# A two-block transformer on one core: memory weights, memory products and the x path reordered in the first phase

## The chip, the cores and the metric

The kernel runs on one core of a Trainium2 chip. The metric is device time in microseconds (us) of one launch, the median of several runs. The core has TensorE (PE in the profile, its weight loads PEld), VectorE (DVE), ScalarE (ACT), GpSimd (POOL) and SyncE (SP), each with a queue of instructions of its own, worked off in order. DMAs are issued from the queues of SP, ACT and POOL.

## What is computed

A transformer layer with two attentions, then two more layers on its output, which also attend to a memory of 256 tokens. All of it in fp32, 512 tokens of 1024 features. What lies in the first phase is only this:

```python
mod = silu(c) @ w_ada + b_ada                     # 6 x 1024 columns
shift_mix, scale_mix, gate_mix, shift_ffn, scale_ffn, gate_ffn = split(mod, 6)
h = rms_norm(x) * (1 + scale_mix) + shift_mix     # 512 x 1024
proj = h @ w_in                                   # 1024 x 3072
...
# for each of two later layers l, from mem (256 x 1024):
kv_l = (rms_norm(mem) * mem_norm_l) @ w_mem_kv_l  # 1024 x 512, keys and values
```

The rest (attentions, output projections, three feed-forward parts with convolutions) is not touched by the change.

## The kernel before, in words

Features lie on the partitions in 8 tiles of 128, tokens on the columns. A matrix product with 32-bit precision is made of three passes: each weight chunk of 128 x 2048 is split into a high part (`w_hi`, by ACT, L1479) and the rest (`w_lo`, by DVE, L1921), the activations likewise into `act_hi` and `act_lo`, and for each tile of inputs PE adds hi*hi, hi*lo and lo*hi (L808 to L810). A chunk is 256 output columns, so 2 output tiles of 8 input tiles, 48 matmuls. The chunks are numbered through the whole kernel; chunk 0 is the first of `w_in`.

The order of the work is written out by hand: each engine has a program, and semaphores say when a step may start. The first phase goes as follows.

- **SP** (L462 to L510) loads `mem`, then half of the small vectors (L439), then `x` in one DMA of 2 MB (L465), then the first 256 columns of the memory weights (`load_mem(0)`, 1 MB, L468). It then waits for the third slab of `w_ada` (`ada_loaded[2]`, L503) and loads chunks 0 and 1 (L457). Chunk 2 goes into a stage that w_ada used, and waits for its first two adds of the second group (`ada_added` of 10, L452).
- **POOL** (L611 to L656) builds the identity, waits until the small vectors are turned and copied (L633), issues four loads of `w_ada` of 1 MB, builds the constants (L638, L647), waits for chunk 0 (L649), issues four more, then parks the scaled memory of both layers in DRAM (2 MB, L655) and loads small things.
- **ACT** squares the two memory tiles (L1683), takes the root, and the silu of `c`. For each of 8 feature tiles of the turned memory it writes two copies out of PSUM, each with the gain of one layer (`mem_scaled`, L1698). The root for x stands between two of them (L1695). Then it copies the 8 turned tiles of x into `x_norm` (L1703), splits chunk 0 (L1479), and makes `act_hi` (L1713).
- **DVE** makes the diagonal matrices of the memory's inverse norms (L2210), waits for `x`, makes its four sums of squares (L2225), the reciprocal (L2270) and four diagonals (L2273). It adds up the first eight parts of `w_ada` (L2238, L2241), sums the turned columns (L2279), adds bias and one (L2282), and from there goes on without a choice: `w_lo` of chunk 0 (L1921), eight `act_lo` (L2289), the memory's keys (L2263), `w_lo` of chunk 1, eight more adds of `w_ada`, a copy of the first output (L2255), `w_lo` of chunk 2, and the shifted activations (L2295). The shift is known only later than the scale: chunks 0 and 1 use the scaled activations, and what the shift adds to them is summed apart (L2371).
- **PE** turns the memory, 8 tiles, by products with the diagonal that also scale it (L1093). Two banks of PSUM are used in turn, so that each tile waits for ACT's copies of the last but one (L1100). It turns x likewise (L1093 again), and waits for the last copy. It does a quarter of the memory's key products (`mem_half`, L1122), turns the columns of `w_ada`'s sums (`ada_sum`, L1073), does the other three quarters, and begins chunk 0 as soon as its weights and the first `act_lo` are there. Inside chunk 1 stands the sum for the shift (L1148), behind it four tiles of the raw x (L1110), behind chunk 2 the vectors of the convolutions (L921).

`mem_half(0, 0)` and `mem_half(0, 1)` are the two tiles of keys for the memory, 16 instructions each.

## Time and profile before

| | us |
|---|---|
| median of 3 runs | 1817.51 (1817.28 to 1817.79) |
| the profiled execution, its own time | 1817.18 |
| its span in the profile | 1815.5 |
| PE busy | 1780.8 (98% of the span) |
| DVE busy | 1096.0 (60%) |
| ACT busy | 733.0 (40%) |
| POOL busy | 40.4 (2%) |

The profile is taken from one execution. The span is from its first to its last instruction; the execution's own time is 1.7 us more. Busy time is what an engine spends in instructions that compute; matmuls overlap, and a matmul's duration is longer than the distance to the next. The first phase, up to the point at which PE has no gap any more, is about 73 us of the 1815.5.

### The profile page before, as it was taken

Reading aid. Unit: us, or ns where it says so; the run is one execution under the profiler, and the core shown is the slowest. Engines: PE = TensorE matmul, PEld = TensorE weight load, DVE = VectorE, ACT = ScalarE, POOL = GpSimd, SP = SyncE. Lnnn points to the kernel's source line nnn. Section 1 sums busy time; section 2 is a strip of 40 time slices with the busy share of each in tenths; the row PEclk is TensorE's granted clock in tenths of the full one; section 3 lists DMA queues with packets and bytes.
Section 4 is the critical chain, followed back from the end, with each engine's and each line's share of the span. In section 5 each row is a group of like instructions: output and inputs, shape, how many; then the busy total and the mean of one; then the engine's idle time right before and its main releaser. Section 6 shows DMA issues by size and latency. Waiting matters only on the chain.

```text
span 1815.5 us, 22458 instructions
## 1 busy us (share of the span) xinstructions
PE 1780.8 (98%) x8312; PEld 1427.9 (79%) x8312; DVE 1096.0 (60%) x1601; ACT 733.0 (40%) x1031; POOL 40.4 (2%) x78
## 2 busy tenths in 40 slices
PE   7999899999999999999999999999999999999998
PEld 6887556788888888878888888889765788888887
DVE  6877675655555335765677674245577567767423
ACT  7313663343344223444334433232365443443322
POOL 4110000000000000000000000000000000000000
PEclk9999999999999999999999999999999999999999
DMA  9793112223322323312322222233401233222231
GB/s 348 268 336 129 47 53 97 77 94 108 99 92 87 106 86 100 109 47 93 114 94 92 92 92 96 95 93 99 163 24 47 70 108 100 92 92 92 93 105 70
DMA packets 149081, 195.29 MB, mean 108 GB/s; under 512 B 3646, under 2 KB 133000, under 8 KB 146332
## 3 DMA queue, kind: packets, MB, share of 16 engines
q1 hardware_dynamic: 141272, 155.28, 26.0%
q0 software_dynamic: 7600, 39.13, 5.8%
q8 instruction: 41, 0.67, 0.2%
q14 instruction: 20, 0.16, 0.0%
q10 hardware_dynamic: 148, 0.05, 0.0%
HBM read 189.15 MB, written 5.29 MB: 107 GB/s over the span
## 4 chain that ended last, share of the span: by engine, by line
PE 91%; DVE 5%; ACT 2%; issue 1%; DMA 1%; ACTq 0%; DVEq 0%
PE bank L808 20%; PE bank L810 20%; PE bank L809 20%; PE bank L871 3%; PE bank L873 2%; PE bank L872 2%; PE bank L1452 2%; PE bank L1453 2%; PE bank L1451 2%; PE bank L995 1%; PE bank L947 1%; PE bank L964 1%; PE bank L851 1%; PE bank L852 1%; PE bank L853 1%
## 5 line engine op out<-in xcount | busy, mean ns | idle before, releaser
L1921 DVE TENSOR_TENSOR w_lo<-w_stage,w_hi 128x2048 fp32r<-128x2048 f32 (+3 forms) x135 | 296.6, 2197 | 439.1 <-ACT w_hi L1479 438.8
L808 PE MATMUL bank<-act_hi,w_hi 128*128 128x512 f32 x1232 | 482.6, 392 | 2.2 <-DVE act_lo L1971 0.7
L810 PE MATMUL bank<-act_hi,w_lo 128*128 128x512 f32 x1232 | 480.0, 390 | 0.0
L809 PE MATMUL bank<-act_lo,w_hi 128*128 128x512 f32 x1232 | 479.9, 390 | 0.0
L1479 ACT ACTIVATE w_hi<-w_stage 128x2048 fp32r<-128x2048 f32 (+3 forms) x137 | 251.7, 1837 | 459.6 <-PE bank L810 334.7
L808 PEld LDWEIGHTS bank<-act_hi,w_hi 128*128 128x128 f32 x1232 | 231.4, 188 | 53.4 <-DVE act_lo L1971 2.3
L810 PEld LDWEIGHTS bank<-act_hi,w_lo 128*128 128x128 f32 x1232 | 231.4, 188 | 48.2
L809 PEld LDWEIGHTS bank<-act_lo,w_hi 128*128 128x128 f32 x1232 | 231.5, 188 | 47.8 <-issue 0.5
L809 PE MATMUL bank<-mid_lo,w_hi 128*128 128x512 f32 x352 | 137.1, 389 | 0.0
L810 PE MATMUL bank<-mid_hi,w_lo 128*128 128x512 f32 x352 | 137.1, 389 | 0.0
L808 PE MATMUL bank<-mid_hi,w_hi 128*128 128x512 f32 x352 | 137.1, 389 | 0.0
L1624 ACT ACTIVATE mid_hi<-tmp 128x512 f32 x66 | 40.7, 633 | 98.4 <-DVE tmp L2131 98.4
L809 PEld LDWEIGHTS bank<-mid_lo,w_hi 128*128 128x128 f32 x352 | 66.1, 188 | 13.8
L808 PEld LDWEIGHTS bank<-mid_hi,w_hi 128*128 128x128 f32 x352 | 66.1, 188 | 13.6
L810 PEld LDWEIGHTS bank<-mid_hi,w_lo 128*128 128x128 f32 x352 | 66.1, 188 | 13.6
L1451 PE MATMUL bank<-w_hi,mid_hi 128*128 128x512 f32 x176 | 68.9, 392 | 0.0
L1453 PE MATMUL bank<-w_lo,mid_hi 128*128 128x512 f32 x176 | 68.6, 390 | 0.0
L1452 PE MATMUL bank<-w_hi,mid_lo 128*128 128x512 f32 x176 | 68.6, 390 | 0.0
L1616 ACT ACTIVATE tmp<-tmp,vec 128x512 f32<-128x512 f32 x44 | 33.5, 809 | 70.0 <-DVE tmp L1943 70.0
L1616 ACT ACTIVATE mid_val<-tmp,vec 128x512 f32 x44 | 33.5, 808 | 69.7 <-DVE tmp L1943 69.7
L1943 DVE SCALAR_TENSOR_TENSOR tmp<-bank,rms 128x512 f32<-128x512 f32 x88 | 56.3, 681 | 0.0
L2135 DVE TENSOR_TENSOR mid_lo<-tmp,mid_hi 128x512 f32 x66 | 42.7, 689 | 9.3 <-ACT mid_hi L1624 9.3
(412 smaller groups left out, 2608.6 us busy)
## 6 DMA issues: line engine op xcount, KB each, us to landing
ada_stage<-in_w_ada POOLq DMA_DIRECT2D x24, 1024.0 KB, 7.6
w_stage<-in_w_up SPq DMA_DIRECT2D x22, 1024.0 KB, 5.0
w_stage<-in_a_ffn_in SPq DMA_DIRECT2D x22, 1024.0 KB, 5.0
w_stage<-in_b_ffn_in SPq DMA_DIRECT2D x22, 1024.0 KB, 5.0
w_stage<-in_w_in SPq DMA_DIRECT2D x10, 1024.0 KB, 7.7
w_stage<-in_b_ffn_out SPq DMA_DIRECT2D x10, 1024.0 KB, 5.1
w_stage<-in_w_down SPq DMA_DIRECT2D x8, 1024.0 KB, 5.1
w_stage<-in_a_ffn_out SPq DMA_DIRECT2D x8, 1024.0 KB, 5.0
```

Of the source, the lines that this page charges most:

```text
L808: pe.matmul(dst, wh, mh, start=start and k == 0, stop=False)
L809: pe.matmul(dst, wh, ml, start=False, stop=False)
L810: last = pe.matmul(dst, wl, mh, start=False, stop=stop and k == nk - 1)
L871: pe.matmul(dst, wh, mh, start=start and k == ks[0], stop=False)
L1451: pe.matmul(dst, mh, hi[:, k, :], start=j == 0 and k == 0, stop=False)
L1452: pe.matmul(dst, ml, hi[:, k, :], start=False, stop=False)
L1453: last = pe.matmul(dst, mh, lo[:, k, :], start=False, stop=j == 5 and k == nk - 1)
L1479: act.activation(w_hi[slot][:, 0:n], raw[:, 0:n], ACT.Copy).then_inc(w_hi_done, 1)
L1616: act.activation(conv_tile(f, i, s, m), conv_src(f, s, m)[:, :], ACT.Identity, scale=w2, bias=b).then_inc(tap_started, 1)
L1921: dve.tensor_tensor(w_lo[slot][:, 0:n], raw[:, 0:n], w_hi[slot][:, 0:n].bitcast(FP32), ALU.subtract).then_inc(w_ready, 1)
L1943: return dve.scalar_tensor_tensor(out=dst, in0=src[:, :], scalar=scale, in1=norm[:, :], op0=ALU.mult, op1=ALU.mult)
L2135: dve.tensor_tensor(mid_lo[:, bass.ds(2 * i + m, 1), :], tmp[:, m, :], mid_hi[:, bass.ds(2 * i + m, 1), :].bitcast(FP32), ALU.subtract).th ...
```

## The change

- **SP**: the first memory weights are loaded ahead of `x`, and `x` comes in two DMAs of 1 MB (tokens 0 to 255, then 256 to 511), each with a semaphore of its own.
- **POOL**: the first four loads of `w_ada` wait for the first half of `x` too.
- **PE**: the memory is turned into banks 0 to 3, two tiles in each, with no wait between them. All memory products (`mem_half`) stand right behind, as soon as layer a's copies are kept. Then x is turned (banks 0 to 3), then the sums of the modulation.
- **ACT and DVE**: DVE keeps the turned memory for layer a (8 multiplies), ACT for layer b (8 activations, tiles 4 to 7 first, then 0 to 3). Each waits for pairs of tiles, and for the other engine where both would read one bank. Of the four sums of squares of x ACT makes two (token tiles 0 and 2), behind its keeping, and DVE two (1 and 3), behind its own. The four diagonals go from DVE to ACT.
- **The first split** (chunk 0) is made in two halves of 1024 columns, which are input tiles 0 to 3 and 4 to 7. PE starts with the first (`w_half`), and waits for the second before the fifth input tile. DVE makes the second half of `w_lo` behind the third `act_lo`.
- The semaphores `x_turned`, `xn_turned` and the memory's part of `tr_ready` become one, `turned`. The scratch for the squares of x moves from `x` to the space of `act_hi`.

```diff
@@ -82,7 +82,7 @@
 CONVS = [("conv_w", "conv_b"), ("a_ffn_conv_2", "a_ffn_conv_b_2"), ("b_ffn_conv_2", "b_ffn_conv_b_2")]
 
 
-BATCHES = [("vec", 1), ("mem", 8), ("conv", 2), ("ws", 1),
+BATCHES = [("vec", 1), ("conv", 2), ("ws", 1),
            ("out", 8)]
 TR0 = {name: sum(n for _, n in BATCHES[:i]) for i, (name, _) in enumerate(BATCHES)}
 
...
@@ -239,7 +239,7 @@
         q_bias = stats[:, 24:28]
         bias_acc = tmp[:, 1, :]
         col_1, col_2, col_12 = stats[:, 36:40], stats[:, 40:44], stats[:, 56:60]
-        x_junk = x[:, 6:8, :].rearrange("p a b -> p (a b)")
+        x_junk = at("x_junk", [P, NT, D], o_act)
         sq = tmp[:, 2:4, :]
 
 
...
@@ -251,6 +251,9 @@
 
         def mem_bank(c, m):
             return (4 + m, 6 + m, 6 + m, 4 + m)[c]
+
+        def xn_bank(k):
+            return bank[k % 4]
 
         def norm_bank(name):
             return bank[6] if name == "oa" else bank[5]
...
@@ -365,12 +367,14 @@
         c_act = sem("c_act")
         mod_summed, mod_added, mod_ready = sem("mod_summed"), sem("mod_added"), sem("mod_ready")
         ada_turned, ada_reduced, kb_saved = sem("ada_turned"), sem("ada_reduced"), sem("kb_saved")
+        mem_kept = [sem(f"mem_kept{l}") for l in range(2)]
+        w_half = sem("w_half")
         mem_ss, mem_root, mem_rms = sem("mem_ss"), sem("mem_root"), sem("mem_rms")
         mem_diag, mem_tile, mem_done, mem_saved = (
             sem("mem_diag"), sem("mem_tile"), sem("mem_done"), sem("mem_saved"))
         w_mem_loaded = [sem(f"w_mem_loaded{c}") for c in range(4)]
         x_squared, x_root, x_inv, x_diag = sem("x_squared"), sem("x_root"), sem("x_inv"), sem("x_diag")
-        xn_turned, xn_saved = sem("xn_turned"), sem("xn_saved")
+        xn_saved = sem("xn_saved")
         v_tile, v_saved = sem("v_tile"), sem("v_saved")
         mem_stored, mem_back = sem("mem_stored"), sem("mem_back")
         mem_parked, mem_unparked = sem("mem_parked"), [sem(f"mem_unparked{l}") for l in range(2)]
...
@@ -462,13 +466,16 @@
             sp.dma_start(mem_tok[:, :, :], a["mem_2"][0].rearrange("(t p) d -> p t d", p=P))\
                 .then_inc(mem_loaded, 16)
             load_vectors(sp, VECTORS[0::2])
-            sp.dma_start(x_tok[:, :, :], a["x"][0].rearrange("(t p) d -> p t d", p=P))\
-                .then_inc(x_loaded, 16)
+
             def load_mem(c):
                 sp.dma_start(w_mem[c][:, :, :], cols(rows("a_w_mem_kv_2"), 0, KT, CHUNK_COLS * c))\
                     .then_inc(w_mem_loaded[c], 16)
 
             load_mem(0)
+            for h in range(2):
+                sp.dma_start(x_tok[:, 2 * h:2 * h + 2, :],
+                             a["x"][0, 2 * P * h:2 * P * (h + 1), :].rearrange("(t p) d -> p t d", p=P))\
+                    .then_inc(x_loaded[h], 16)
 
             def stream(ph, w, pairs):
 
...
@@ -631,6 +638,7 @@
             pool.memset(eps, EPS).then_inc(consts_set, 1)
             pool.memset(one_col, 1.0).then_inc(consts_set, 1)
             pool.wait_ge(tr_saved, TR0["vec"] + 1)
+            pool.wait_ge(x_loaded[0], 16)
             for n in range(4):
                 ada(n, first[n])
             ones = [(neg_upper, -1.0), (tri, 1.0), (strict_neg, 0.0), (causal_neg, 0.0), (ident_b, 0.0)]
...
@@ -786,9 +795,12 @@
         @block.tensor
         def _(pe):
             def chunk(c, slot, nk, ncol, moving, g=None, gslot=0, start=True, stop=True, n=SEQ,
-                      k0=0, tile_wait=None, chunk_wait=None, between=None, inside=None):
-
-                pe.wait_ge(w_ready, c + 1)
+                      k0=0, tile_wait=None, chunk_wait=None, between=None, inside=None, halves=False):
+
+                if halves:
+                    pe.wait_ge(w_half, 2)
+                else:
+                    pe.wait_ge(w_ready, c + 1)
                 if start and (not isinstance(g, int) or g >= 2):
                     pe.wait_ge(group_free, g - 1)
                 if chunk_wait:
...
@@ -1095,12 +1109,10 @@
 
             pe.wait_ge(mem_diag, 2)
             for k in range(KT):
-                n = TR0["mem"] + k
-                if n >= 2:
-                    pe.wait_ge(tr_saved, n - 1)
                 for t in range(2):
-                    last = scaled_turn(bank[6 + n % 2], mem_tok[:, t, P * k:P * (k + 1)], NT + t)
-                last.then_inc(tr_ready, 1)
+                    last = scaled_turn(bank[k // 2][:, NMEM * (k % 2):NMEM * (k % 2) + NMEM],
+                                       mem_tok[:, t, P * k:P * (k + 1)], NT + t)
+                last.then_inc(turned, 1)
 
             def turn_x(tiles):
                 for k in tiles:
...
@@ -1109,7 +1121,7 @@
                     for t in range(NT):
                         last = pe.transpose(bank[4 + k % 4][:, P * t:P * (t + 1)],
                                             x_tok[:, t, P * k:P * (k + 1)], ident[:, :])
-                    last.then_inc(x_turned, 1)
+                    last.then_inc(turned, 1)
 
             def mem_half(c, m, ks=range(KT)):
                 l = c // 2
...
@@ -1125,23 +1137,22 @@
                     last.then_inc(mem_done if m else mem_tile, 1)
 
 
+            pe.wait_ge(mem_kept[0], KT)
+            pe.wait_ge(w_mem_loaded[0], 16)
+            mem_half(0, 0)
+            mem_half(0, 1)
             pe.wait_ge(x_diag, NT)
+            pe.wait_ge(mem_kept[1], KT)
             for k in range(KT):
-                if k == 2:
-                    pe.wait_ge(tr_saved, TR0["mem"] + KT)
                 if k >= 4:
                     pe.wait_ge(xn_saved, k - 3)
                 for t in range(NT):
-                    last = scaled_turn(bank[4 + k % 4], x_tok[:, t, P * k:P * (k + 1)], t)
-                last.then_inc(xn_turned, 1)
+                    last = scaled_turn(xn_bank(k), x_tok[:, t, P * k:P * (k + 1)], t)
+                last.then_inc(turned, 1)
             pe.wait_ge(xn_saved, KT)
-            pe.wait_ge(w_mem_loaded[0], 16)
-            mem_half(0, 0, range(4))
             pe.wait_ge(consts_set, 14)
             pe.wait_ge(ada_added, 8)
             ada_sum(range(8, 16), 2)
-            mem_half(0, 0, range(4, KT))
-            mem_half(0, 1)
             def shift_sum():
                 pe.wait_ge(ada_added, 16)
                 pe.wait_ge(group_free, G0["qk_a"] + 1)
...
@@ -1151,7 +1162,7 @@
                 chunk(C0["qk_a"] + j, j % 2, KT, CHUNK_COLS, act, g=G0["qk_a"] + j, gslot=j % 2,
                       tile_wait=normed(("w_in_scaled", "", "w_in", "")[j]) if j % 2 == 0 else None,
                       chunk_wait=(scaled, SPLIT0["w_in_scaled"] + 8) if j == 1 else None,
-                      inside=shift_sum if j == 1 else None)
+                      inside=shift_sum if j == 1 else None, halves=j == 0)
                 if j == 1:
                     pe.wait_ge(mem_saved, 1)
                     turn_x(range(4))
...
@@ -1689,25 +1700,42 @@
             act.wait_ge(tr_saved, TR0["vec"] + 1)
             act.activation(sig_c, vec[:, VEC0["c"]:VEC0["c"] + 8], ACT.Silu).then_inc(c_act, 1)
             act.preload_act_table(ACT.Sqrt)
+            def keep_mem_b(k):
+                act.wait_ge(turned, 2 * (k // 2) + 2)
+                if k < 4:
+                    act.wait_ge(mem_kept[0], 2 * (k // 2) + 2)
+                act.activation(mem_scaled[:, 1, k, :], bank[k // 2][:, NMEM * (k % 2):NMEM * (k % 2) + NMEM],
+                               ACT.Copy, scale=gain("b_mem_norm_2", k)).then_inc(mem_kept[1], 1)
+
             for k in range(KT):
-                if k == 6:
-                    act.wait_ge(x_squared, NT)
-                    act.activation(x_rms, x_ss, ACT.Sqrt, scale=1.0 / D, bias=eps).then_inc(x_root, 1)
-                act.wait_ge(tr_ready, TR0["mem"] + k + 1)
-                for l, name in enumerate(("a_mem_norm_2", "b_mem_norm_2")):
-                    last = act.activation(mem_scaled[:, l, k, :], bank[6 + (TR0["mem"] + k) % 2][:, 0:NMEM],
-                                          ACT.Copy, scale=gain(name, k))
-                last.then_inc(tr_saved, 1)
+                keep_mem_b((k + 4) % KT)
+            for t in (0, 2):
+                act.wait_ge(x_loaded[t // 2], 16)
+                act.activation(x_junk[:, t, :], x_tok[:, t, :], ACT.Square, accum_out=x_ss[:, t:t + 1])\
+                    .then_inc(x_squared, 1)
+            act.wait_ge(x_squared, NT)
+            act.activation(x_rms, x_ss, ACT.Sqrt, scale=1.0 / D, bias=eps).then_inc(x_root, 1)
+            act.wait_ge(x_inv, 1)
+            for t in range(NT):
+                act.activation(diag[:, t, :], ident[:, :], ACT.Copy, scale=x_rms[:, t:t + 1]).then_inc(x_diag, 1)
+
+            def save_xn(k):
+                act.wait_ge(turned, KT + k + 1)
+                act.activation(x_norm[:, k, :], xn_bank(k)[:, :], ACT.Copy).then_inc(xn_saved, 1)
+
             for k in range(KT):
-                act.wait_ge(xn_turned, k + 1)
-                act.activation(x_norm[:, k, :], bank[4 + k % 4][:, :], ACT.Copy).then_inc(xn_saved, 1)
+                save_xn(k)
+            act.wait_ge(xn_saved, KT)
 
             def save_x(tiles):
                 for k in tiles:
-                    act.wait_ge(x_turned, k + 1)
+                    act.wait_ge(turned, 2 * KT + k + 1)
                     act.activation(x[:, k, :], bank[4 + k % 4][:, :], ACT.Copy).then_inc(x_saved, 1)
 
-            split_at(0)
+            act.wait_ge(w_loaded[0], 16)
+            for half, done in ((0, w_half), (1, w_hi_done)):
+                act.activation(w_hi[0][:, 1024 * half:1024 * half + 1024],
+                               w_stage[0][:, 1024 * half:1024 * half + 1024], ACT.Copy).then_inc(done, 1)
             act.wait_ge(scaled, SPLIT0["w_in_scaled"] + 8)
             for t in range(KT):
                 act.activation(act_hi[:, t, :], x_norm[:, t, :], ACT.Copy, scale=modv(SCALE_MIX, t))\
...
@@ -2216,13 +2244,16 @@
             last.then_inc(tr_saved, 1)
             dve.wait_ge(tr_saved, TR0["vec"] + 1)
             dve.tensor_tensor(gain_a1, vec[:, VEC0["final_g"]:VEC0["final_g"] + 8],
-                              vec[:, VEC0["a_norm1_2"]:VEC0["a_norm1_2"] + 8], ALU.mult)\
-                .then_inc(gain_a1_set, 1)
-            dve.wait_ge(x_loaded, 16)
-            for t in range(NT):
-                if t:
-                    dve.wait_ge(x_squared, t)
-                dve.tensor_tensor_reduce(out=x_junk, in0=x_tok[:, t, :], in1=x_tok[:, t, :], scale=1.0,
+                              vec[:, VEC0["a_norm1_2"]:VEC0["a_norm1_2"] + 8], ALU.mult)
+            for k in range(KT):
+                dve.wait_ge(turned, 2 * (k // 2) + 2)
+                if k >= 4:
+                    dve.wait_ge(mem_kept[1], 2 * (k // 2) - 2)
+                dve.tensor_scalar(mem_scaled[:, 0, k, :], bank[k // 2][:, NMEM * (k % 2):NMEM * (k % 2) + NMEM],
+                                  gain("a_mem_norm_2", k), None, ALU.mult).then_inc(mem_kept[0], 1)
+            for t in (1, 3):
+                dve.wait_ge(x_loaded[t // 2], 16)
+                dve.tensor_tensor_reduce(out=x_junk[:, t, :], in0=x_tok[:, t, :], in1=x_tok[:, t, :], scale=1.0,
                                          scalar=0.0, op0=ALU.mult, op1=ALU.add,
                                          accum_out=x_ss[:, t:t + 1]).then_inc(x_squared, 1)
 
...
@@ -2268,10 +2299,6 @@
 
             dve.wait_ge(x_root, 1)
             dve.reciprocal(x_rms, x_rms).then_inc(x_inv, 1)
-            dve.wait_ge(x_inv, 1)
-            for t in range(NT):
-                dve.tensor_scalar(diag[:, t, :], ident[:, :], x_rms[:, t:t + 1], None, ALU.mult)\
-                    .then_inc(x_diag, 1)
             dve.wait_ge(c_act, 1)
             for n in range(4):
                 ada_first(n)
...
@@ -2281,7 +2308,13 @@
             dve.wait_ge(mod_added, 1)
             dve.scalar_tensor_tensor(out=mod[:, 8:16], in0=mod[:, 8:16], scalar=1.0, in1=vec[:, P + 8:P + 16],
                                      op0=ALU.add, op1=ALU.add).then_inc(scaled, 8)
-            split_w(0, 0)
+            def split_first(half):
+                dve.wait_ge(w_hi_done if half else w_half, 1)
+                part = slice(1024 * half, 1024 * half + 1024)
+                dve.tensor_tensor(w_lo[0][:, part], w_stage[0][:, part], w_hi[0][:, part].bitcast(FP32),
+                                  ALU.subtract).then_inc(w_ready if half else w_half, 1)
+
+            split_first(0)
             dve.wait_ge(scaled, SPLIT0["w_in_scaled"] + 8)
 
             def low_scaled(t):
...
@@ -2306,6 +2339,8 @@
 
             for t in range(KT):
                 low_scaled(t)
+                if t == 2:
+                    split_first(1)
             mem_group(0)
             split_w(1, 1)
             for n in range(4, 8):
```

## Rows read from the trace of the kernel before

**Rows 1.** Windows: us, length, busy (x instructions) of PE, PEld, DVE, ACT, POOL, clock, DMA.
```profile
30.00:40.00 10.00, 10.00 (x48) 8.57 (x47) 9.54 (x14) 9.79 (x13) 9.96 (x18) 1.00 0.92 344
...
100.00:130.00 30.00, 30.00 (x134) 24.87 (x133) 21.55 (x13) 4.79 (x3) 3.17 (x6) 1.00 1.00 363
```

**Rows 2.** Chain that ended last, 0 to 130 us: start, us, what.
```profile
44.23 8.99 DMA ada_stage<-in_w_in
```

**Rows 3.** Timeline of PE, 8 to 73 us: start, us, what.
```profile
9.50 2.07 PE L1093 MATMUL bank<-diag,mem_tok 128*128 128x128 f32 x8 [0.62 <-DVE diag L2210]
12.45 6.07 PE L1093 MATMUL bank<-diag,mem_tok 128*128 128x128 f32 x24 [0.88 <-ACT mem_scaled L1698]
19.05 7.41 PE L1093 MATMUL bank<-diag,x_tok 128*128 128x128 f32 x64 [0.53 <-DVE diag L2273]
27.15 2.00 PE L1122 MATMUL bank<-mem_scaled,w_mem 128*128 128x256 f32 x8 [0.69 <-ACT x_norm L1703]
29.25 1.07 PE L1073 MATMUL bank<-ident,ada_acc 128*128 128x128 f32 x8
30.15 5.35 PE L1122 MATMUL bank<-mem_scaled,w_mem 128*128 128x256 f32 x24
35.14 0.58 PE L808 MATMUL bank<-act_hi,w_hi 128*128 128x512 f32 x1
...
37.41 0.39 PE L808 MATMUL bank<-act_hi,w_hi 128*128 128x512 f32 x1
...
60.51 0.47 PE L808 MATMUL bank<-act_hi,w_hi 128*128 128x512 f32 x1 [0.57 <-DVE act_lo L2295]
...
71.51 0.62 PE L921 MATMUL bank<-ident,vec_rows 88*128 88x88 f32 x6
72.46 0.47 PE L808 MATMUL bank<-act_hi,w_hi 128*128 128x512 f32 x1 [0.33 <-DVE qkv L2255]
```

**Rows 4.** Timeline of DVE, 8 to 56 us.
```profile
12.51 1.22 DVE L2225 CUSTOM_DVE_ANT_0 x_res<-x_tok 128x1024 f32<-128x1024 f32 x1 [2.58 <-DMA x_tok<-in_x]
...
17.90 0.18 DVE L2270 RECIPROCAL stats<-stats 128x4 f32<-128x4 f32 x1 [0.36 <-ACT stats L1695]
...
18.91 0.75 DVE L2238 TENSOR_SCALAR ada_acc<-ada_stage,stats 128x1024 f32<-128x1024 f32 x1
19.69 9.41 DVE L2241 SCALAR_TENSOR_TENSOR ada_acc<-ada_stage,stats,ada_acc 128x1024 f32<-128x1024 f32 x7
...
31.77 2.28 DVE L1921 TENSOR_TENSOR w_lo<-w_stage,w_hi 128x2048 fp32r<-128x2048 f32 x1
33.97 5.38 DVE L2289 SCALAR_TENSOR_TENSOR act_lo<-x_norm,vec,act_hi 128x512 fp32r<-128x512 f32 x8
39.28 0.74 DVE L2263 COPY kmT<-bank 128x256 f32<-128x256 f32 x2
...
55.20 2.29 DVE L1921 TENSOR_TENSOR w_lo<-ada_stage,w_hi 128x2048 fp32r<-128x2048 f32 x1 [1.21 <-ACT w_hi L1479]
```

**Rows 5.** Timeline of ACT, 5 to 45 us.
```profile
7.25 1.06 ACT L1683 ACTIVATE sq_junk<-mem_tok 128x1024 f32<-128x1024 f32 x1
...
13.71 1.69 ACT L1698 ACTIVATE mem_scaled<-bank,vec 128x256 f32<-128x256 f32 x4 [0.58 <-PE bank L1093]
...
17.57 0.30 ACT L1695 ACTIVATE stats<-stats 128x4 f32<-128x4 f32 x1
...
29.77 1.91 ACT L1479 ACTIVATE w_hi<-w_stage 128x2048 fp32r<-128x2048 f32 x1 [2.68 <-DMA w_stage<-in_w_in]
```

**Rows 6.** DMA issues from 3.5 to 5 us: KB each, median us to landing.
```profile
x_tok<-in_x SPq DMA_DIRECT2D x1, 2048.0 KB, 8.7
w_mem<-in_a_w_mem_kv SPq DMA_DIRECT2D x1, 1024.0 KB, 12.9
```

**Rows 7.** PE matmuls of mem_tok: groups by form, 9 to 17.75 us; then by tile.
```profile
L1093 PE MATMUL bank<-diag,mem_tok 128*128 128x128 f32 x28 | 7.5, 444 | 1.7 <-ACT mem_scaled L1698 0.9 <-DVE diag L2210 0.6
...
L1093 PE MATMUL bank<-diag,mem_tok x32: 275/422/583, 9.5 to 18.2; 128*128 128x128 f32 x32
```

10 lines of the change are left out of this document (6 added, 4 removed).

## The prediction

> **What bounds the kernel now.** Read the windows first: from 100 to 130 us TensorE has no gap, from 30 to 40 it is already full [rows 1]. Whatever starts the stream of 512-column products earlier or later therefore moves the end, unless a later wait takes it up. The only such place nearby is in the chain of waits: the load of the third weight chunk, 44.23 to 53.22 us [rows 2].
>
> Then the timeline of TensorE [rows 3]: memory tiles turned from 9.50 to 18.52 with gaps, x turned from 19.05 to 26.46, a quarter of the memory products, the sums of the modulation at 29.25, the other three quarters from 30.15, the first chunk at 35.14. At 60.51 the third chunk starts after 0.57 of waiting for act_lo, and at 72.46 the fourth after 0.33 of waiting for a copy by VectorE.
>
> The timeline of VectorE [rows 4] says what 29.25 waited for: the eight adds of w_ada, which run without a gap from 18.91 to 29.10. Then come reduction, w_lo of the first chunk (31.77), act_lo (33.97) and so on without a pause until 53.99; then 1.21 us of idle before w_lo at 55.20. So two chains, VectorE's and TensorE's, lie within a microsecond of each other. The end moves only by what both are late, less these idle times.
>
> **The change, part by part.** I take four engine queues in their new order.
>
> *Turning the memory.* The same 32 instructions go to four banks, without waiting for ScalarE. Their pace depends on TensorE's clock. 28 of them, begun before 17.75, average 444 ns; the fastest, after it, takes 275 [rows 7]. That is the low level (1.2 GHz) against the high one (2.4). At the low level the pace is (2.07 - 0.58) / 7 = 0.213 us, at the high one 7.41 / 64 = 0.116 [rows 3, 7]. The windows' column calls the granted clock 1.00 in both [rows 1], so durations decide here. In the old order the rise came at 17.8, after a stream with gaps. The new stream has no gap, so 17.8 is the late end; the early end is 9.5, the high level from the first turn on. Neither row is nearer, and I take the middle, 13.65. By then 19 have begun; the other 13 take 1.5. The sixth tile is ready at 14.5, the eighth at 15.4.
>
> *Keeping it.* ScalarE takes all eight tiles for layer b, beginning with the fifth, at 1.69 / 4 = 0.42 each [rows 5]: tiles 5 and 6 until 15.35, 7 and 8 until 16.25, 1 to 4 until 17.95. VectorE takes eight for layer a. A multiply of 128x256 out of PSUM isn't in the trace; the copy of that size is, 0.74 for two [rows 4], and the bound above is ScalarE's 0.42. At 0.37, behind ScalarE's pair in the same bank, the last two end at 17.0. At the upper bound it is 17.1.
>
> *Memory products.* All 32 now come before x is turned. At 5.35 / 24 = 0.223 [rows 3] they take 7.1: 17.05 to 24.15. They fill some idle time, but most of them now stand before a step on the path.
>
> *Squares of x.* These wait behind the keeping. VectorE's two take 2 x 1.26 (four had 12.51 to 17.54 [rows 4]): 17.0 to 19.5. ScalarE's two take 1.18 each (7.25 to 8.40 is one [rows 5]): 17.95 to 20.3. Root and reciprocal add 0.55 (17.57 to 18.1 [rows 4, 5]), so the adds of w_ada begin at 20.9, not 18.91. VectorE saves the four diagonals, 0.8 between 18.08 and 18.91, and that is already in it. The adds take 10.2 and end at 31.1. The four diagonals on ScalarE have no row: between 0.3 (the root, four columns) and 0.42 (256 columns) each [rows 5], done by 22.6, covered by the memory products until 24.15.
>
> *Turning x.* 8.1 from the first turn to TensorE free again (19.05 to 27.15, with ScalarE's last save [rows 3]): 24.15 to 32.25. The sums of the modulation therefore begin at 32.2, not 29.25: **2.95 late**, and TensorE is now what is last (w_ada is ready at 31.1).
>
> *First split in halves.* VectorE's work until the fourth act_lo is the same: w_lo of 2.20 (31.77 to 33.97) and four at 5.38 / 8 = 0.67. In the old order the fourth was there at 36.66 and TensorE asked for it at 37.41 [rows 3, 4], with 0.75 to spare, because the memory products had held the start until 35.14. In the new one it comes at 36.66 + 2.95 = 39.6 and TensorE, which starts at 36.55 (a half of w_lo saved), stands before it at 38.8. So the halving starts the first product 1.1 earlier and gives back 0.8 at the fourth tile. From there TensorE is 2.95 - 0.7 = 2.25 late.
>
> *What takes it up.* VectorE is 2.95 late from act_lo on, and the 1.21 of idle before 55.20 goes: 1.75. TensorE is 2.25 late, and the wait of 0.57 before 60.51 goes: 1.7. Both meet at the third chunk; the fourth is again tied to VectorE's copy [rows 3]. **Sum: +1.75 us.** Nothing later has slack for it: TensorE is full.
>
> *Transfers.* x and the memory weights landed 12.46 and 17.1 us in [rows 6]. In the new order the second megabyte in SyncE's queue is the first half of x. So it lands near 12.5, and the last half by 17.1, before 19.1, where ScalarE wants it. GpSimd's four loads of w_ada wait for the first half, 12.6 instead of 10.03. Behind them on GpSimd's queue stand the constants, wanted only at 32.2. The bounds are no delay (the bus had the same volume) and 2.6 in full. Even then the fourth slab, used in the old order at 26.5, is wanted at 28.6. The first weights, landed before 29.77 [rows 5], come at 32.4 at the latest, and ScalarE is free for them at 32.2. The parking of the memory is needed at 55. Cost 0, up to the third chunk's load, which is a rival below.
>
> **How the numbers follow.** The profiled run has a span of 1815.5, 1.7 around it, 0.3 below the median. 1815.5 + 1.75 = 1817.25, with 1.7 and 0.3 around it 1819.3. A microsecond on the start of the sums is a microsecond on the end, above a delay of 1.2. The rise at 17.8 gives 33.6, so +3.15; at 9.5 it gives 30.3, so 0. Less than 0.2% (3.6 us) counts as no change.
>
> **The rivals.**
> - *A, slower: the clock is still low when the memory products begin.* They then stand at 18.45, after a pause of 1.7 for the keeping, and each costs 0.22 more. With eight of 32 at the low level: 4.35 + 1.8 - 1.2 = +4.95, 1822.5; with all 32, 1827.7. It decides from the third slow product on. For it: 28 turns ran low in the trace [rows 7]. Against: the stream is denser. 0.13.
> - *B: the third weight chunk lands late.* It is asked for 2.95 later, at 47.2, and VectorE can take it from 56.95, so it decides when the load takes over 7.8. The row says 8.99 [rows 2], but beside the parking, which is nearly over by then. Landed at 56.2, VectorE is 2.95 late: +2.95, 1820.5. 0.17.
> - *C: nothing moves.* With the clock high from the start the sums begin 1.05 late and all of it is taken up: 1817.5. 0.12.
> - *D: halves of x land one after another with their full latency.* The Trainium skill (DMA: Bandwidth & Descriptors, Bandwidth) gives 6.15 us for one megabyte alone and asks for at least that size. By an estimate from this page, x would be there at 24.5 and the end come near +6. The trace has three megabytes in 11.1 us behind the first [rows 6], 3.7 each, overlapped, so it speaks against this rule here. From rows, D is a last half that lands after 19.1, at one for one: at 22 the adds begin at 23.7 and end at 33.9, +3.45, 1821.0. 0.04.
> - *E, faster.* The products that held the start at 35.14 are gone, and if the squares were done by 18 the sums could begin where they did; both chains would then gain at most the 0.5 between act_lo at 34.65 and 35.14, and again lose it to the load of rows 2. Over 0.2% I see no mechanism: 0.04, within it part of C.
> The forecast (+0.8 to +3.2) has 0.50. Faster 0.04, same 0.79, slower 0.17 (A, half of the tail of D, part of B). The range reaches from C, 1817.2, to most of A, 1822.4.
>
> **What would show it.** Right: x turned only from about 24 on, the sums of the modulation at 31.5 to 33.6, TensorE last before them; VectorE idle before the reduction; the fourth act_lo waited for in the first chunk; no idle of VectorE before the third w_lo; 72.46 moved by 1.75. Wrong: x turned before 22, or the sums before 30.5.

## The result, and the profile after

| us | before | changed |
|---|---|---|
| median of 21 runs each | 1817.67 | 1821.59 |
| lowest, highest | 1816.83, 1820.39 | 1819.67, 1823.83 |
| ratio, 95% interval | | 1.002 [1.0014, 1.0026] |
| span of the profiled execution | 1815.5 | 1817.8 |

Slower by 3.9 us, just above the 3.6 that was called a change. The profiled span is only 2.3 longer. The 21 times fall into two groups with nothing between: a first of ten from 1819.67 to 1820.35, an upper one of eleven from 1821.59 to 1823.83. The median is the lowest time of the upper group, so one run more in the first group would have put it near 1820.4. The profile is of the first group.

One run of all that follow, in e3_no_pool_wait, took 2684.23 us at a mean granted clock of 0.62; it enters no comparison, and its cause is not known.

TensorE's timeline in it, to be laid beside [rows 3]:

```profile
9.53 5.25 PE L1107 MATMUL bank<-diag,mem_tok 128*128 128x128 f32 x32 [0.33 <-DVE diag L2238]
16.70 7.17 PE L1134 MATMUL bank<-mem_scaled,w_mem 128*128 128x256 f32 x32 [1.91 <-DVE mem_scaled L2252]
23.71 7.31 PE L1107 MATMUL bank<-diag,x_tok 128*128 128x128 f32 x64
31.70 1.10 PE L1087 MATMUL bank<-ident,ada_acc 128*128 128x128 f32 x8 [0.69 <-ACT x_norm L1724]
36.29 0.65 PE L822 MATMUL bank<-act_hi,w_hi 128*128 128x512 f32 x1 [3.49 <-DVE act_lo L2322]
...
40.01 0.39 PE L822 MATMUL bank<-act_hi,w_hi 128*128 128x512 f32 x1
...
60.67 1.91 PE L1122 MATMUL bank<-ident,x_tok 128*128 128x128 f32 x16
62.84 0.47 PE L822 MATMUL bank<-act_hi,w_hi 128*128 128x512 f32 x1 [0.25 <-DVE act_lo L2328]
...
74.79 0.47 PE L822 MATMUL bank<-act_hi,w_hi 128*128 128x512 f32 x1 [0.34 <-DVE qkv L2286]
```

The memory is turned without gaps, the products stand at 16.70, x follows at 23.71 (19.05 before), and the sums of the modulation begin at 31.70, 2.45 late. Then comes what the kernel before does not have: 3.49 us of idle before the first chunk at 36.29. Up to 39.7 the products behind it take 0.63 each, with 0.43 from one to the next; from 40.01 on they take 0.39, 0.23 apart. The fourth tile's product begins at 40.01 against 37.41, and the fourth chunk at 74.79 against 72.46: 2.33 late.

The third chunk, where the kernel before had waited 0.57, still waits 0.25. Ahead of it TensorE turns four tiles of the raw x, from 60.67 on. The same step in the kernel before:

```profile
58.03 1.91 PE L1110 MATMUL bank<-ident,x_tok 128*128 128x128 f32 x16
```

So TensorE ends its second chunk 2.64 late, and the 0.57 of waiting would have left 2.07 of that. VectorE's timeline, beside [rows 4]:

```profile
11.65 0.88 DVE L2252 TENSOR_SCALAR mem_scaled<-bank,vec 128x256 f32<-128x256 f32 x2 [1.69 <-PE bank L1107]
...
19.66 0.75 DVE L2269 TENSOR_SCALAR ada_acc<-ada_stage,stats 128x1024 f32<-128x1024 f32 x1
...
34.26 1.22 DVE L2314 TENSOR_TENSOR w_lo<-w_stage,w_hi 128x1024 fp32r<-128x1024 f32 x1
...
37.39 1.22 DVE L2314 TENSOR_TENSOR w_lo<-w_stage,w_hi 128x1024 fp32r<-128x1024 f32 x1
38.52 3.40 DVE L2322 SCALAR_TENSOR_TENSOR act_lo<-x_norm,vec,act_hi 128x512 fp32r<-128x512 f32 x5
...
57.52 2.29 DVE L1949 TENSOR_TENSOR w_lo<-ada_stage,w_hi 128x2048 fp32r<-128x2048 f32 x1 [0.96 <-ACT w_hi L1490]
```

The adds of w_ada begin at 19.66 (18.91 before) and end at 30.16, so they were not what the sums waited for. The halves of w_lo are there (34.26, 37.39). The fourth act_lo is ready at 39.2, before TensorE wants it. And VectorE still stands idle before the third w_lo, 0.96 at 57.52.

GpSimd's loads of w_ada, and the third weight chunk in the chain of waits, beside [rows 2]:

```profile
13.88 3.00 POOL L618 DMA_DIRECT2D ada_stage<-in_w_ada  x4 [12.26 <-DMA x_tok<-in_x]
...
31.93 2.85 POOL L618 DMA_DIRECT2D ada_stage<-in_w_ada  x4 [11.36 <-DMA w_stage<-in_w_in]
```

```profile
46.80 8.75 DMA ada_stage<-in_w_in
```

The first four are issued at 13.88 instead of 10.03, the next four at 31.93 instead of 30.04. The third weight chunk is asked for at 46.80 instead of 44.23 and lands at 55.55 instead of 53.22.

Two chains meet at the third chunk. One is the transfer: load, w_hi, w_lo, sum of the shift, `act_hi`, `act_lo`. From the landing to TensorE's third chunk it is 7.29 us in both profiles (60.51 less 53.22, 62.84 less 55.55). The other is TensorE itself, whose second chunk must be done before `act_hi` can be written again. ScalarE's `act_hi` shows which came last; here it was the sum (L2338), so the transfer:

```profile
61.18 5.02 ACT L1756 ACTIVATE act_hi<-x_norm,vec 128x512 fp32r<-128x512 f32 x8 [3.69 <-DVE vec L2338]
```

The landing is 2.33 late and so is the fourth chunk; TensorE alone would have made it 2.07.

### The profile page after: what moved, and what is told of

The parts are those of the page before. It is cut to its first block, busy times and chain, and to the rows that moved or that the text cites. A ratio compares the mean times of both kernels' runs of the same rounds, so it can differ in the third digit from the quotient of the medians.

```text
span 1817.8 us, 22473 instructions
## 1 busy us (share of the span) xinstructions
PE 1779.6 (98%) x8312; PEld 1426.0 (78%) x8312; DVE 1096.4 (60%) x1602; ACT 733.2 (40%) x1032; POOL 39.0 (2%) x78
## 4 chain that ended last, share of the span: by engine, by line
PE 91%; DVE 5%; ACT 2%; issue 1%; DMA 1%; ACTq 0%; DVEq 0%
PE bank L822 20%; PE bank L824 20%; PE bank L823 20%; PE bank L885 3%; PE bank L887 2%; PE bank L886 2%; PE bank L1464 2%; PE bank L1463 2%; PE bank L1462 2%; PE bank L1009 1%; PE bank L961 1%; PE bank L978 1%; PE bank L865 1%; PE bank L866 1%; PE bank L867 1%; PE bank L1060 1%
## 5 line engine op out<-in xcount | busy, mean ns | idle before, releaser
L1949 DVE TENSOR_TENSOR w_lo<-w_stage,w_hi 128x2048 fp32r<-128x2048 f32 (+2 forms) x134 | 294.5, 2197 | 439.8 <-ACT w_hi L1490 439.6
```

The costliest lines, as they stand in the source:

```text
L1949: dve.tensor_tensor(w_lo[slot][:, 0:n], raw[:, 0:n], w_hi[slot][:, 0:n].bitcast(FP32), ALU.subtract).then_inc(w_ready, 1)
```

## The experiments

Theories: the **queue** (memory products ahead of the turning of x make the sums late), the **transfers** (everything from w_ada on lands later), the **clock** (new idle stretches of TensorE let its clock fall, in some executions more than in others). "Fourth chunk" is its first product in the profiled execution: 72.46 before, 72.19 in another execution of the kernel before (1816.86). The number behind a label is the median. None of the experiments differs from the kernel before by 2%, and "late" always means against the first profile of the kernel before.

**r0_changed**: the changed kernel once more, no edit.

> The changed kernel again, beside the others on one chip. If the spread of its times (1819.7 to 1823.8 in the first result) belongs to the kernel, it comes back: some runs near 1820, others 2 to 4 us above, median 3 to 4 us over the kernel before. If it belonged to that chip, the median is about 2.3 over (the difference of the two profiled spans) and the runs lie within 1 us.

1822.58, ratio 1.0023 [1.0014, 1.0031]. Four runs from 1819.53 to 1820.29, seven from 1822.51 to 1823.71: the groups belong to the kernel. The profiled one, of the first group, has its fourth chunk at 74.41.

**e1_half_behind**

```diff
             mem_half(0, 0)
-            mem_half(0, 1)
             pe.wait_ge(x_diag, NT)
...
             ada_sum(range(8, 16), 2)
+            mem_half(0, 1)
```

> The changed kernel with the second half of the memory products (16 instructions, 3.6 us) put back behind the sums of the modulation. Queue theory (the products stand before the turning of x and make it late): x is turned from 21.1, when its diagonals are there, not from 23.7; the sums begin at 30.2, when the adds of w_ada end, not at 31.7. Clock theory (TensorE's 3.5 us of idle before the first chunk lets its clock fall, and how much of the next work runs low differs from run to run): the idle is gone, no product of the first chunk takes 0.63, and the runs lie within 1 us of each other near 1820. Transfer theory (the third weight chunk lands at 55.5 because all transfers from w_ada on are 1.7 to 1.9 late): the profiled fourth chunk still starts at 74.4 to 74.8. If the queue alone made the loss, it starts at 73.2 and the median falls to about 1818.5.

1820.36, ratio 1.0014 [1.0006, 1.0023], from 1818.91 to 1822.68: one broad group. TensorE's timeline:

```profile
17.83 5.41 PE L1134 MATMUL bank<-mem_scaled,w_mem 128*128 128x256 f32 x16 [1.91 <-DVE mem_scaled L2252]
...
31.12 1.07 PE L1087 MATMUL bank<-ident,ada_acc 128*128 128x128 f32 x8 [0.73 <-ACT x_norm L1724]
...
73.81 0.47 PE L822 MATMUL bank<-act_hi,w_hi 128*128 128x512 f32 x1 [0.34 <-DVE qkv L2286]
```

Sixteen products took 5.41, not the 3.6 they take later in the same run, so x was turned two microseconds later than expected and the sums began at 31.12, not 30.2. This is the first sight of the low clock in the memory products. The expectation named only the idle before the first chunk; there no product took 0.63, but the spread stayed; the pause of 1.91 ahead of the products was still there. The fourth chunk at 73.81 is below the 74.4 expected by the transfers alone. Its load was asked for at 46.17 and landed at 54.56, a microsecond earlier than in the changed kernel, and the fourth chunk is late by the same 1.35 as the landing.

**e2_keep_busy**

```diff
             ada_sum(range(8, 16), 2)
+            for n in range(14):
+                pe.transpose(bank[6 + n // 7][:, 0:P], ident[:, :], ident[:, :])
```

> The changed kernel with 14 turns of the identity, whose output nobody reads, in TensorE's idle before the first chunk (3.1 us at the high level); all else as it is. Clock theory: the first products take 0.39, not 0.63, all runs lie near 1820 (within 1 us), and the median is 1 to 2 us under the changed kernel's, though work was added. Queue and transfer theory alone: nothing changes in time or in spread, since both chains are later at the third chunk (the profiled fourth chunk at 74.7 as now).

1821.83, ratio 1.0018 [1.0009, 1.0027], 1819.98 to 1822.63. A miss as it was built: the 14 turns took 1.69, not 3.1, and left 1.96 of idle:

```profile
33.03 1.69 PE L1157 MATMUL bank<-ident 128*128 128x128 f32 x14
36.68 0.47 PE L822 MATMUL bank<-act_hi,w_hi 128*128 128x512 f32 x1 [1.96 <-DVE act_lo L2324]
...
37.83 0.63 PE L823 MATMUL bank<-act_lo,w_hi 128*128 128x512 f32 x1
```

The first three products ran high, the next ones low. It neither showed the clock theory nor refuted it: the times are one range up to 1822.63, not two groups, but the median fell by 0.75 only.

**e3_no_pool_wait**

```diff
             pool.wait_ge(tr_saved, TR0["vec"] + 1)
-            pool.wait_ge(x_loaded[0], 16)
```

> The changed kernel without GpSimd's wait for the first half of x ahead of the four loads of w_ada (issued at about 10.0, not 13.9). Transfer theory: the slabs land up to 1.7 us earlier, the first weights before 30, the third weight chunk near 53.8, VectorE has no idle before the third w_lo (0.96 now) and the fourth chunk starts at 73.8: 0.9 us gained. If the transfers cost nothing, as the prediction had it, the fourth chunk stays at 74.7. The other side: x's second half then shares the bus with w_ada and lands after 17, and the squares and with them the adds start up to 1 us later.

1819.97, ratio 1.0014 [1.0006, 1.0023]. That median counts the run of 2684.23; the other eleven have 1819.88, and eight of them lie from 1819.64 to 1820.19. VectorE's third w_lo, and ScalarE's act_hi for the third chunk:

```profile
57.02 2.27 DVE L1948 TENSOR_TENSOR w_lo<-ada_stage,w_hi 128x2048 fp32r<-128x2048 f32 x1
```

```profile
61.45 5.02 ACT L1755 ACTIVATE act_hi<-x_norm,vec 128x512 fp32r<-128x512 f32 x8 [5.83 <-PE bank L823]
```

VectorE has no idle before w_lo any more, as expected: the load landed near 53.7, 0.45 late, though it was asked for at 47.33, 3.1 late. So GpSimd's wait for x is what made the landing late in the changed kernel. But the profiled fourth chunk, at 75.05, did not come forward: act_hi for the third chunk also waits until TensorE has finished the second, and TensorE was 3.2 late there (its clock fell before the first chunk, as in the changed kernel). This tie between the chains was not in the prediction. Whether more runs fell into the first group by this edit or by chance stays open.

**e7_fill_both**

```diff
+            for n in range(8):
+                pe.transpose(bank[7][:, 0:P], ident[:, :], ident[:, :])
             pe.wait_ge(mem_kept[0], KT)
...
             ada_sum(range(8, 16), 2)
+            for n in range(28):
+                pe.transpose(bank[6 + n // 14][:, 0:P], ident[:, :], ident[:, :])
```

> The changed kernel with TensorE kept busy in both of its new idle stretches by turns of the identity whose output nobody reads: 8 between the turning of the memory and the memory products (1.91 us of idle now), 28 between the sums of the modulation and the first chunk (3.49 us; 14 of them took 1.69). Clock theory: no product of the memory and of the first chunk runs at the low level's pace, and the upper group of times (1822.5 to 1823.7, 7 of 11 runs) is gone: all runs between 1819.4 and 1820.6. The profiled fourth chunk stays at 74.4 to 74.8, since VectorE and the third weight load are there as late. If the two groups have another cause, they stay and the median is 1822 or more.

1819.92, ratio 1.0011 [1.0002, 1.002]. All eleven runs from 1819.76 to 1820.33. Adding 36 instructions that compute nothing took 2.7 us off the median and the upper group away.

```profile
17.39 7.17 PE L1134 MATMUL bank<-mem_scaled,w_mem 128*128 128x256 f32 x32 [1.04 <-DVE mem_scaled L2256]
...
36.98 0.47 PE L822 MATMUL bank<-act_hi,w_hi 128*128 128x512 f32 x1 [0.43 <-DVE act_lo L2326]
...
40.01 0.50 PE L822 MATMUL bank<-act_hi,w_hi 128*128 128x512 f32 x1 [0.72 <-DVE act_lo L2326]
...
74.86 0.47 PE L822 MATMUL bank<-act_hi,w_hi 128*128 128x512 f32 x1 [0.33 <-DVE qkv L2290]
```

The products take 7.17, no product of the first chunk takes 0.63, and now the wait for the fourth tile shows (0.72 at 40.01) that the prediction had put there. The fourth chunk, 74.86, is as late as in the changed kernel. The rise of the clock came as late here as in executions of the upper group (the memory was turned in 6.13 us, see below), and still the products ran high. l1_look, of the same series and the same chip, took 1823.59 without the fillers. So the idle ahead of the products lets the clock fall, the clock is the difference between the groups, and queue and transfers are what is left. Which of the two fillers did it was not tried by itself; the next profiles point to the first.

**l1_look, l3_look_changed**: two more executions of the changed kernel.

> One more execution of the changed kernel, to find one of the upper group in a profile. Clock theory: if its time is above 1822, more of its first chunk or of its memory products runs at the low level's pace (0.43 for a 512-column product, not 0.23) than in the two profiles of the lower group (9 of the first 10 products). If its time is near 1820, it looks like these.

> A further execution of the changed kernel. Clock theory: above 1822, the windows show the low level (near 0.5) in the memory products and at the start of the first chunk, as in the slow profile (sums at 34.3); near 1820, the products run high (sums at 31.6 to 31.8) and only the start of the first chunk is low.

1823.59 and 1822.55, both of the upper group. TensorE in the first:

```profile
9.52 6.18 PE L1107 MATMUL bank<-diag,mem_tok 128*128 128x128 f32 x32 [0.34 <-DVE diag L2238]
17.62 8.86 PE L1134 MATMUL bank<-mem_scaled,w_mem 128*128 128x256 f32 x32 [1.92 <-DVE mem_scaled L2252]
...
34.31 1.10 PE L1087 MATMUL bank<-ident,ada_acc 128*128 128x128 f32 x8 [0.69 <-ACT x_norm L1724]
38.89 0.77 PE L822 MATMUL bank<-act_hi,w_hi 128*128 128x512 f32 x1 [3.48 <-DVE act_lo L2322]
...
76.89 0.47 PE L822 MATMUL bank<-act_hi,w_hi 128*128 128x512 f32 x1 [0.36 <-DVE qkv L2286]
```

and in the second:

```profile
18.05 8.86 PE L1134 MATMUL bank<-mem_scaled,w_mem 128*128 128x256 f32 x32 [1.91 <-DVE mem_scaled L2252]
```

The 32 products took 8.86 in both, 1.7 more than the 7.17 of the first group; the sums began at 34.31 and 34.74, the fourth chunk at 76.89 and 77.56. The windows name the clock (us, length, busy, granted clock, DMA share, GB/s). In the first, l1_look:

```profile
18.00:20.00 2.00, 2.00 (x6) 0.50 1.02 420
...
38.00:40.00 2.00, 1.11 (x3) 0.59 1.04 420
40.00:42.00 2.00, 2.00 (x7) 0.55 1.08 383
```

and at the same places in the first group's profile:

```profile
18.00:20.00 2.00, 2.00 (x11) 1.00 1.02 420
...
36.00:38.00 2.00, 1.71 (x4) 0.60 1.03 424
38.00:40.00 2.00, 2.00 (x6) 0.54 1.03 424
```

0.50 is the low level (1.2 GHz): only the upper group has it in the products, both have it at the start of the first chunk. TensorE had stood idle for 1.9 before the products in both, but had turned the memory in 5.25 and 5.44 us in the profiles of the first group, and in 6.18 and 6.64 in the upper one, where the clock had risen later. The other versions with that same pause fall in line: after 5.88 (e2) and 5.76 (e3) the products ran high, after 6.58 (e1) and 6.44 (e8) low. So of the eight profiles with the pause unfilled the four with the shorter turnings ran high and the four with the longer ones low.

In the upper group the third chunk waits for TensorE and not for the transfer, as ScalarE shows in l1_look:

```profile
63.27 5.02 ACT L1756 ACTIVATE act_hi<-x_norm,vec 128x512 fp32r<-128x512 f32 x8 [6.12 <-PE bank L824]
```

l1_look has one more low stretch, far behind the change:

```profile
280.00:284.00 4.00, 4.00 (x9) 0.59 0.00 0
```

TensorE had waited 1.68 there for VectorE in the stick-breaking attention. The four products behind the wait, in l1_look:

```profile
279.97 2.23 PE L1060 MATMUL bank<-sb_pl,neg_upper 128*128 128x384 f32 x4 [1.68 <-DVE sb_pl L2493]
```

and in the first group's profile, after the same wait:

```profile
277.81 1.56 PE L1060 MATMUL bank<-sb_pl,neg_upper 128*128 128x384 f32 x4 [1.68 <-DVE sb_pl L2493]
```

Behind the fourth chunk l1_look takes 1744.6 us (span less its start); eleven of the fourteen profiles, of all kernels, take 1742.9 to 1743.1.

**e5_products_ahead**: the kernel before, with the products' place alone changed.

```diff
+            pe.wait_ge(tr_saved, TR0["mem"] + KT)
+            pe.wait_ge(w_mem_loaded[0], 16)
+            mem_half(0, 0)
+            mem_half(0, 1)
             pe.wait_ge(x_diag, NT)
...
-                    last = scaled_turn(bank[4 + k % 4], x_tok[:, t, P * k:P * (k + 1)], t)
+                    last = scaled_turn(bank[k % 4], x_tok[:, t, P * k:P * (k + 1)], t)
```

(ACT's saves of x_norm read `bank[k % 4]` too; the products behind x are gone.)

> The kernel before with one part of the change alone: all memory products ahead of the turning of x (x is turned into banks 0 to 3 for that). Queue theory: products from 19.7, when the memory is kept, to 26.8; x turned until 34.1, TensorE free again at 34.9; the sums begin at 34.9, not 29.25, 5.65 late; the fourth chunk starts about 4.4 late (76.9), median about 1822. Clock theory adds 0 to 3 in single runs, for a new idle of 3.5 before the first chunk. If the products' place costs nothing, as the idle of TensorE before x suggests, the median stays near 1817.7.

1825.24, ratio 1.0036 [1.0022, 1.005], over five runs.

```profile
19.38 8.74 PE L1122 MATMUL bank<-mem_scaled,w_mem 128*128 128x256 f32 x32 [1.39 <-ACT mem_scaled L1696]
...
35.95 1.10 PE L1073 MATMUL bank<-ident,ada_acc 128*128 128x128 f32 x8 [0.69 <-ACT x_norm L1701]
...
80.53 0.47 PE L808 MATMUL bank<-act_hi,w_hi 128*128 128x512 f32 x1 [0.31 <-DVE qkv L2253]
```

Sums 6.7 late. The queue alone was to give 5.65; the products took 8.74 instead of 7.1, the clock's part. The fourth chunk came 8.1 late and not 4.4: behind an idle of 4.56 the first ten products of the first chunk took 0.63 to 0.76 us, not 0.39.

**e6_transfers**: the kernel before, with memory weights ahead of x, x in halves, and GpSimd's wait.

```diff
+            for h in range(2):
+                sp.dma_start(x_tok[:, 2 * h:2 * h + 2, :],
+                             a["x"][0, 2 * P * h:2 * P * (h + 1), :].rearrange("(t p) d -> p t d", p=P))\
+                    .then_inc(x_loaded[h], 16)
...
+            pool.wait_ge(x_loaded[0], 16)
```

> The kernel before with the order of the transfers alone: memory weights ahead of x, x in two halves, the first four loads of w_ada behind the first half. Transfer theory: w_ada lands 1.7 later, the first weights at 31.5, the third weight chunk at 55.0 instead of 53.2 though it is asked for at nearly the same time (44.2 plus at most 0.8 for the later squares); VectorE's idle before the third w_lo grows from 1.2 to about 2.5, and the fourth chunk starts at 74.0, 1.5 late: median near 1819.3. The prediction had 0 for the transfers by themselves: 1817.7.

1819.19, ratio 1.0007 [0.9998, 1.0016].

```profile
56.54 2.29 DVE L1924 TENSOR_TENSOR w_lo<-ada_stage,w_hi 128x2048 fp32r<-128x2048 f32 x1 [1.03 <-ACT w_hi L1482]
```

```profile
30.26 1.06 PE L1076 MATMUL bank<-ident,ada_acc 128*128 128x128 f32 x8
...
73.81 0.47 PE L811 MATMUL bank<-act_hi,w_hi 128*128 128x512 f32 x1 [0.33 <-DVE qkv L2258]
```

The third w_lo begins at 56.54 (55.20 before), although VectorE was free at 55.5, and the fourth chunk at 73.81, 1.35 late; expected were 1.5. The sums begin at 30.26, 1.0 late: the squares began at 13.04 (12.51 before) and the diagonals of x, made behind them, were ready at 20.0, so TensorE turned x from 20.05 on (19.05 before). The third weight chunk was asked for at 45.76, 1.53 late, and landed 1.35 late; the load itself took no longer than before (8.8 us, 9.0 before). The interval reaches 1; the profile's 1.35 is what the verdict rests on.

**e8_split_whole**: the changed kernel, first split whole (`split_w(0, 0)` on VectorE, one activation on ScalarE, no `halves`).

> The changed kernel with the first weight split whole again; all else as it is. The prediction's step on the halves: the first product starts 1.1 us later after the sums, the wait before the fourth tile of inputs is gone, and TensorE ends the chunk within 0.2 us of the changed kernel's; no change in time beyond the two groups. If the halves gain what they save on the start, the first chunk ends 1.1 later. In the first chunk of an execution with a low clock the halves can even hide part of it, since TensorE would have waited for the fourth tile.

1823.43, ratio 1.0026 [1.0015, 1.0036], lowest 1821.36.

```profile
34.55 1.09 PE L1087 MATMUL bank<-ident,ada_acc 128*128 128x128 f32 x8 [0.69 <-ACT x_norm L1724]
40.19 0.77 PE L822 MATMUL bank<-act_hi,w_hi 128*128 128x512 f32 x1 [4.55 <-DVE act_lo L2320]
...
79.41 0.47 PE L822 MATMUL bank<-act_hi,w_hi 128*128 128x512 f32 x1 [0.34 <-DVE qkv L2284]
```

A miss. From the sums to the first product 5.64, against 4.58 in l1_look: 1.06, as worked out. But to the fourth chunk it is 44.86 against 42.58 and 42.82 in l1_look and l3_look_changed, so the whole split costs 2.0 to 2.3 here, not 0.2. The idle before the chunk grew to 4.55, and twelve of its products took 0.63 or more, where l1_look has six and l3_look_changed seven. Even its lowest run is 1.8 above the changed kernel's.

**e9_half_filled**: e1 and e3 together, with 12 turns of the identity before the first half of the products and 4 behind it.

> The candidate from what the runs showed: half of the memory products behind the sums, no wait of GpSimd for x, and 12 plus 4 turns of the identity that keep TensorE busy before and after the first half of the products. Queue, transfer and clock theory together: x turned from about 21.1, sums at 30.2 to 30.8, no product low, third weight chunk near 53.5, fourth chunk at 72.9 to 73.4: one group of times, median 1818.2 to 1818.9, 1 us better than the filled kernel, and still not under the kernel before (1817.7), because the adds of w_ada still begin 0.8 later. If it is under 1817.5, something in the first phase is cheaper than the profiles say.

1819.28, ratio 1.0008 [0.9999, 1.0017], 1818.06 to 1821.51.

```profile
17.20 3.72 PE L1133 MATMUL bank<-mem_scaled,w_mem 128*128 128x256 f32 x16 [0.61 <-DVE mem_scaled L2255]
...
72.78 0.47 PE L821 MATMUL bank<-act_hi,w_hi 128*128 128x512 f32 x1 [0.34 <-DVE qkv L2289]
```

The fourth chunk is only 0.32 late, 2.0 better than in the changed kernel, and no memory product ran low. The rest of the expectation was missed: the median lies above 1818.9, and the times spread over 3.5 us. But behind it this execution takes 1744.7, as l1_look did, and for the same reason:

```profile
275.87 2.50 PE L1059 MATMUL bank<-sb_pl,neg_upper 128*128 128x384 f32 x4 [1.68 <-DVE sb_pl L2496]
```

So 1.7 of its span comes from a place that the change does not touch. Whether that is the whole spread was not seen. No version beat the kernel before.

**l2_look_before**: one more execution of the kernel before.

> One more execution of the kernel before. Its fourth chunk starts at 72.3 to 72.8 in any case, since TensorE has no idle of over 0.9 us ahead of it after the clock's rise. If the time is above 1819, the clock theory puts the low stretch not in the first phase but in the stick-breaking attention, where TensorE waits 1.7 us at a time (as at 280 us in the slow profile of the changed kernel).

1816.86, its fourth chunk at 72.19. Behind it it takes 1742.9. It was none of those above 1819, so where the kernel before loses up to 3 us in some executions was not seen and stays open.

**What ends at the third chunk, in all profiles.** How late is each (us): TensorE's end of the second chunk less the 0.57 that it could wait, ScalarE's w_hi behind the landing of the third weight chunk, and the fourth chunk:

| | TensorE, less 0.57 | transfer | fourth chunk |
|---|---|---|---|
| changed, first group | 2.07 | **2.32** | 2.33 |
| r0_changed, first group | **1.96** | 1.95 | 1.95 |
| l1_look, upper group | **4.42** | 1.98 | 4.43 |
| l3_look_changed, upper group | **5.10** | 1.76 | 5.10 |
| l2_look_before | **-0.26** | -0.63 | -0.27 |
| e1_half_behind | 0.93 | **1.34** | 1.35 |
| e2_keep_busy | 2.48 | **3.01** | 3.02 |
| e3_no_pool_wait | **2.60** | 0.45 | 2.59 |
| e5_products_ahead | **8.07** | 3.01 | 8.07 |
| e6_transfers | 0.56 | **1.34** | 1.35 |
| e7_fill_both | 2.21 | **2.39** | 2.40 |
| e8_split_whole | **6.95** | 1.45 | 6.95 |
| e9_half_filled | 0.28 | **0.30** | 0.32 |

The later of the two is the fourth chunk's delay in every row, to 0.02 us. So the first group of the changed kernel is bound by the transfer or by both, and the upper group by TensorE. e3 took the transfer's delay away alone, and in its profile TensorE's took its place.

## Why the prediction was right, and where it was not

The direction and the range held: 1821.59 in 1817.2 to 1822.4, likeliest 1819.3. That the range held is in part luck. The median fell on the lowest time of the upper group, and the same kernel in r0_changed has 1822.58, outside the range. The delay is 3.9 against 1.75 forecast, just above the 0.2% that was given 0.79 to stay under. What the main sum lacked stood among the rivals: the first group of times is rival B, the upper one rival A, which had 0.17 and 0.13.

- **Products ahead of x: right.** The sums were to begin at 32.2 and began at 31.70. They were bound by TensorE, as said; w_ada was ready at 30.16 (31.1 forecast, since ScalarE began keeping at 13.93 and not 14.5 and took 3.19 and not 3.4). e5 shows this part alone.
- **Keeping: price too low.** VectorE's multiply out of PSUM took 0.44, above both ends given (0.37, 0.42). That made the pause before the products 1.91, not 1.65.
- **Halves: right for a high clock, wrong here.** "The halving starts the first product 1.1 earlier": 1.06. "Gives back 0.8 at the fourth tile": it does where TensorE is kept busy (0.72 in e7). In the changed kernel TensorE reached that tile at 40.01, behind its act_lo, because its first eight products took 0.63 to 0.65. The prediction had TensorE idle from 33.3 to 36.55 in its own times and did not ask what the clock does in it. TensorE was 2.6 late from there on, not 2.25, though the sums were 0.5 earlier than forecast. From the first product to the turning of the raw x it is 24.38 us, 23.83 in e7, so the low stretch cost 0.55. In the profile of the first group this did not decide: the transfer was later still (2.33 against 2.07).
- **What takes it up: the step of the sum that failed.** The prediction let the 1.21 of VectorE's idle before the third w_lo swallow as much of the delay: "no idle of VectorE before the third w_lo". It stayed, 0.96. That idle is a wait for a load which is asked for only when VectorE has made two adds of the second group, so the load came late with VectorE (46.80, 2.57 late) and took 8.75. By the forecast's own rule, sums 2.45 late less 1.2, the end would have been 1.25 late; it was 2.33. That this lies near 1.75 is luck: the sums were 0.5 earlier than forecast, and 1.1 less was taken up.
- **Rival B is the first group.** It was to decide when the load took over 7.8. It took 8.75, and 0.95 of idle is what its rule leaves. It said +2.95; the request came 0.38 earlier and the load was 0.24 shorter than it assumed, which gives the 2.33.
- **"Cost 0" for the transfers: wrong, with 1.35 by themselves (e6).** The first half of x was put near 12.5, and GpSimd's loads at 12.6; they were issued at 13.88. The bounds for w_ada (0 to 2.6) held. Its four late uses were asked about, and the fifth, the third weight chunk, was left to rival B. The landing does not follow the request alone: in e3, without GpSimd's wait, the load was asked for 3.1 late and landed 0.45 late, in l3_look_changed 5.6 and 1.8. What else stood ahead of it was not traced.
- **Outside the span** lie 0.35 more (1819.53 less 1817.5 is 2.0, 1.7 before). All four profiles of the changed kernel have 2.0 to 2.1 there; no run says why.
- **Rival A is the upper group.** It was priced at 1822.5 with eight of the products low. In l1_look and l3_look_changed the low stretch cost 1.7 in the products, with a later rise in the turning ahead of them; l3_look_changed took 1822.55. In one point the mechanism differs: the clock was not "still low" when the products began, in l1_look seven memory tiles' turns began in the last 0.7 us of the turning, at the high level's pace, and behind the pause of 1.9 the granted clock was 0.50. With the pause partly filled, in e7, it stayed at 1.00. Its chance was given as 0.13. It was there in 11 of 21 and 7 of 11 runs (taking the upper group for it, as these two profiles say), and this is why the median is 2.3 us above the forecast.
- Rivals C, D and E did not occur; x's second half was squared from 17.70 on.

## What to carry to other kernels

Work moved into an engine's idle time is free only if that idle time lies behind the step which the path needs; here 7.2 us of products stood in front of the turning of x and made the sums of the modulation 2.45 late. A plan that makes TensorE wait must price the pause twice, once as time and once as the clock of what follows it. And a transfer that is hidden for its first users has to be followed to its last one: the third weight chunk, landing some 40 us later, was where it showed. An idle stretch that waits for a transfer is slack only if the transfer is not itself asked for by the work that is late.

## What the runs showed of the hardware

- One program had two groups of times, 2 to 4 us apart, and the profiles put the difference down to the clock. After 1.9 us of idle the products ran at the low level (0.50) in the two profiles of the upper group and at the high one in the two of the first group. What differed ahead of the idle was the turning of the memory: 6.18 and 6.64 us against 5.25 and 5.44. After 3.49 us of idle the next products ran low in all four, in r0_changed after two that took 0.47 and 0.59 us.
- Instructions that compute nothing made the kernel faster: 1822.58 without them, 1819.92 with 36 of them, and a spread of 0.6 instead of 4.2 us (two series on two chips, the kernel before at 1817.86 and 1818.03; on the second chip l1_look took 1823.59 without them).
- Every profile has the wait of 1.68 for VectorE some 200 us behind the change; in two of fourteen the low level followed it (2.23 and 2.50 for four products instead of 1.56) and cost 1.6 and 1.7 us. The kernel before has that wait too, so this may be a part of its own scatter; no profile of it caught one.
